# Moving the small tables of a one-core transformer kernel so that the two operands of its split matrix products start at addresses with related remainders

## What is computed

```python
# first kind, twice
proj = rmsnorm(x) @ w_in                       # 1024 -> 4896
y = attention parts of proj
x = x + (gated y @ w_o_fox, w_o_nsa) @ w_out
x = x + square(relu(rmsnorm(x) @ w_up)) @ w_down   # 1024 -> 4096 -> 1024
# second kind, twice (even: MLA + GLA heads; odd: grouped-query heads)
h = x @ w_in_even   or   x @ w_in_odd
x = layer_norm(alpha * x + mixer(h) @ w_o)
ffn = 16 experts of width 1024, each on 64 chosen tokens
ple = sigmoid(x @ ple_gate_w + b) * (p @ ple_w)
x = layer_norm(alpha * x + ffn + ple)
```

## Time and profile before

| what | value |
|---|---|
| median of 3 runs | 3397.64 us |
| the profiled execution, its own time | 3401.32 us |
| its span, first to last instruction | 3399.5 us |
| PE busy | 3210.6 us, 94% of the span |
| DVE, ACT, POOL busy | 38%, 28%, 7% |
| mean granted TensorE clock | 0.975 of full speed |

### The profile page before, as it was taken

The page is one execution under the profiler, slowest core; times in us unless marked ns, Lnnn a source line. Parts: engine busy times, 40 slices in busy tenths (PEclk is TensorE's granted clock), DMA queues, the critical chain, the costliest instruction groups (busy, mean ns, idle before and its releaser), DMA issues. The chain is left out here.

```text
span 3399.5 us, 39981 instructions
## 1 busy us (share of the span) xinstructions
PE 3210.6 (94%) x16110; PEld 2170.6 (64%) x16110; DVE 1286.3 (38%) x1773; ACT 958.2 (28%) x1570; POOL 236.9 (7%) x361
## 2 busy tenths in 40 slices
PE   7999999999999999999997899999997999999996
PEld 5886678888787667888786465444436556544442
DVE  4425554242532564333366552111116655111112
ACT  3325433132422633323242521000004542100001
POOL 1004200000100410000000200000000320000000
PEclk9999999999999999999997999999998999999999
DMA  5310123321441022323211235999992113799997
GB/s 158 119 55 26 66 85 98 99 87 62 130 137 38 1 88 86 99 88 98 77 49 23 76 112 218 426 427 427 427 422 86 64 54 118 304 426 427 427 427 308
DMA packets 234295, 590.22 MB, mean 174 GB/s; under 512 B 42962, under 2 KB 146328, under 8 KB 184996
## 3 DMA queue, kind: packets, MB, share of 16 engines
q1 hardware_dynamic: 234148, 588.15, 45.8%
HBM read 581.81 MB, written 2.10 MB: 172 GB/s over the span
## 5 line engine op out<-in xcount | busy, mean ns | idle before, releaser
L2574 PE MATMUL ps<-w_ring,xe 128*64 128x512 f32 x1024 | 233.7, 602 | 18.8 <-DMA w_ring<-in_w 13.8
L422 DVE TENSOR_TENSOR mlp_w_lo<-w_ring,mlp_w_hi 128x2048 fp32r<-128x2048 f32 x62 | 142.1, 2292 | 212.7 <-ACT mlp_w_hi L382 212.7
L357 PE MATMUL ps<-h_hi,in_w_hi 128*128 128x512 f32 (+1 forms) x528 | 207.0, 392 | 2.7 <-DVE h_lo L430 2.7
L357 PE MATMUL ps<-h_lo,in_w_hi 128*128 128x512 f32 (+1 forms) x528 | 205.7, 390 | 0.0
L357 PE MATMUL ps<-h_hi,in_w_lo 128*128 128x512 f32 (+1 forms) x528 | 205.6, 389 | 0.0
L357 PE MATMUL ps<-h_hi,mlp_w_hi 128*128 128x512 f32 x512 | 202.6, 396 | 2.1 <-DVE h_lo L430 2.1
L357 PE MATMUL ps<-h_hi,mlp_w_lo 128*128 128x512 f32 x512 | 202.5, 396 | 0.0
L357 PE MATMUL ps<-h_lo,mlp_w_hi 128*128 128x512 f32 x512 | 202.5, 395 | 0.0
L357 PE MATMUL ps<-mlp_w_hi,u_lo 128*128 128x512 f32 x512 | 202.3, 395 | 0.0
L357 PE MATMUL ps<-mlp_w_lo,u_hi 128*128 128x512 f32 x512 | 202.2, 395 | 0.0
L357 PE MATMUL ps<-mlp_w_hi,u_hi 128*128 128x512 f32 x512 | 202.2, 395 | 0.0
(11 more groups left out here) (551 smaller groups left out, 6153.2 us busy)
## 6 DMA issues: line engine op xcount, KB each, us to landing
ex_front<-in_w SPq DMA_DIRECT2D x192, 1024.0 KB, 17.5
w_ring<-in_w SPq DMA_DIRECT2D x128, 1024.0 KB, 20.7
ex_back<-in_w SPq DMA_DIRECT2D x64, 1024.0 KB, 19.8
w_ring<-in_w_in SPq DMA_DIRECT2D x32, 1024.0 KB, 5.4
w_ring<-in_w_up SPq DMA_DIRECT2D x32, 1024.0 KB, 5.4
w_ring<-in_w_down SPq DMA_DIRECT2D x32, 1024.0 KB, 5.0
w_ring<-in_cmp_w SPq DMA_DIRECT2D x16, 512.0 KB, 5.0
w_ring<-in_w_out SPq DMA_DIRECT2D x8, 1024.0 KB, 6.0
```

The costliest lines, as they stand in the source:

```text
L357: mm = pe.matmul(ps[0:o.rows, bank[k], 0:o.cols], lhsT, rhs, start=(o.first and j == 0), stop=(o.final and j == len(o.mm) - 1))
L422: dve.tensor_tensor(w.lo[:, home(n), 0:used], ring.slots[:, n % RING, 0:used], w.hi[:, home(n), 0:used].bitcast(F32), ALU.subtract).then_i ...
L2574: mm = pe.matmul(ps[rows, bank + half, :], lhsT, slot(2 * m + a)[:, kk, 512 * half:512 * half + 512], start=(k == 0), stop=(k == DC - 1))
```

## The change

Small tables are padded or put together into one tensor, so that the large pairs behind them start elsewhere. In the lines quoted as in the diff: `n2_tables` grows from 32 to 2048 bytes; the even layer's small tables become slices of one tensor of 512 bytes, `e_small`; the odd layer's become slices of one of 2048 bytes, `o_small`; a tensor that nothing uses, `rw_gap` of 192 bytes, is put ahead of `pl_w`. No instruction is added, removed or moved on any engine; the operands have other addresses.

```diff
@@ block1_layer
-        gain = ctx.enter_context(sbuf(nc, "n2_tables", [P, DC], F32))
-        gemm(nc, "mlp", ps, ring, tiles, 2, nxt, rms_flips(C, I["norm_mlp"][l], h, ring, gain[:, :]), side=tail)
+        gain = ctx.enter_context(sbuf(nc, "n2_tables", [P, BANK], F32))
+        gemm(nc, "mlp", ps, ring, tiles, 2, nxt, rms_flips(C, I["norm_mlp"][l], h, ring, gain[:, 0:DC]), side=tail)
@@ even_beside
-    gw, gb, reset = sb("gw", [2 * GRANK, 2, 256]), sb("gb", [P, 2, 2]), sb("la_reset", [P, T])
+    gw, gb, reset = sb("gw", [2 * GRANK, 2, 256]), small[:, 32:36].rearrange("p (d c) -> p d c", d=2), sb("la_reset", [P, T])
...
-    tot, dec = sb("tot", [P, 2, 2, T // GC]), sb("dec", [P, 2, 2, T // GC])
+    tot, dec = (small[:, c:c + 32].rearrange("p (c d n) -> p c d n", c=2, d=2) for c in (64, 96))
@@ even_mixer
-            gains, add, back = sb("mla_g", [P, 3], c2), sb("add2", [P, 3, 2], c2), sb("back2", [2, 3, P], c2)
+            small, back = sb("e_small", [P, P], c2), sb("back2", [2, 3, P], c2)
+            gains, add, gain = small[:, 0:3], small[:, 8:14].rearrange("p (n m) -> p n m", m=2), small[:, 16:16 + DC]
...
-                gain = sb("nf_gain", [P, DC], c3)
@@ heads_beside
-    gains, ones, back = sb("gqa_g", [P, 2]), sb("add3", [P, 4]), sb("back3", [8, 4, P])
+    small, back = sb("o_small", [P, BANK]), sb("back3", [8, 4, P])
+    gains, ones, rk = small[:, 0:2], small[:, 4:8], small[:, 32:64].rearrange("p (i h) -> p i h", i=TT)
...
-    rk, rs = sb("on_rk", [P, TT, 8]), pair(nc, ctx, "on_rs", [8, T])
+    rs = pair(nc, ctx, "on_rs", [8, T])
@@ route_beside
     rws = pair(nc, ctx, f"rws{i}", [P, DC, NE])
+    sb("rw_gap", [P, 48])
```

More of the change, by code:

```diff
@@ L1441, in _, with even_beside @@
                     pe.matmul(ps[:, 1 + n % 7, :], back_r[:, n, :], rs.lo[:, :], start=False, stop=True).then_inc(s.spread, 1)
-def even_beside(nc, ctx, ps, C, I, x, ring, n_split, cq, ckv, cs, gq, gk, lr, og, gains, add, back):
+def even_beside(nc, ctx, ps, C, I, x, ring, n_split, cq, ckv, cs, gq, gk, lr, og, small, gains, add, back):
     def sb(name, shape, dt=F32):
@@ L1928, in even_mixer @@
             gv, gr, lr = sb("gv", [P, TT, 512], c2), sb("gr", [P, TT, 512], c2), sb("lr", [2 * GRANK, T], c2)
-            side = even_beside(nc, c2, ps, C, I, x, ring, lambda n: 4 + n, cq, ckv, cs, gq, gk, lr, og, gains, add, back)
+            side = even_beside(nc, c2, ps, C, I, x, ring, lambda n: 4 + n, cq, ckv, cs, gq, gk, lr, og, small, gains, add, back)
             with ExitStack() as c3:
@@ L1949, in even_mixer @@
                 tiles += [tokens(E[n] + 256 * m, dst[:, :, 256 * m:256 * m + 256]) for n, dst in (("gv", gv), ("gr", gr)) for m in range(2)]
-                gain = sb("nf_gain", [P, DC], c3)
                 with nc.allow_non_contiguous_dma("narrow columns"):
-                    gemm(nc, "ei", ps, ring, tiles, 2, lead=rms_flips(C, I["norm_final"], h, ring, gain[:, :]), also=tables,
+                    gemm(nc, "ei", ps, ring, tiles, 2, lead=rms_flips(C, I["norm_final"], h, ring, gain), also=tables,
                          side=side, banks=4)
```

## The result

The changed kernel takes 3375.86 us (median of 7 runs, 3368.91 to 3382.67), the kernel before 3397.64 us (7 runs). The ratio is 0.9935, with a 95% interval of 0.9922 to 0.9948: 21.8 us, 0.65%, faster, and clear of the half per cent that the prediction set as its bound.

The account below looks back on a forecast made before the run. The prediction took PE, busy 94% of the span, as the bound; 20.3 + 1.2 - 1.3 + 0.6 - 0.2 + 1.2 = 21.8 us saved from 3397.64 gave 3376 us. The range was 3366 to 3390.

Parts of the forecast that it names:

- the half per cent that the prediction set as its bound: Whole kernel: a measurement can tell about 0.5%, 17.0 us, from no change.
- PE bounds mlp, and its pace is the distance of the operands: mlp: PE busy 358.58 of 358.60 us; 233.3 ns a matmul at distance 32 falls to 226.7 at 0.
- The term of 20.3 us: mlp, two layers: 3072 matmuls each save 233.3 - 226.7 ns once n2_tables is padded, 20.3 us.
- upper bound, 21.8 us: mlp: the most its 3072 matmuls could save, taking wy's 226.2 ns as the aligned pace.
- the first rival: Whole kernel: distance doesn't matter, mlp's 233.3 ns has another cause, time stays at 3398 us; chance 0.08.
- ei about nothing: ei: from distance 32 to 0, wide matmuls save 1.2 us and narrow ones lose 1.3.
- oi and pl: oi: wide matmuls save 0.6 us, narrow ones lose 0.2; pl: saves 1.2 us, bounds 0 and 1.2.
- The partial case, 229.1 ns in mlp: mlp and ei fall only to the pace of oi and pl: 12.2 us saved, 3385 us; chance 0.08.
- No effect: Whole kernel: operand distance doesn't matter at all, the time stays at 3398 us; chance 0.08.
- the slower case: Narrow matmuls lose 1.3 us in ei and 0.2 in oi, mlp gains nothing: 3399 us; chance 0.03.
- Clock by chance, carried by the range: Between stages: pauses of PE lower the granted clock and may shift; the range carries the runs' 13.4 us spread.
- The two small terms that were too large: oi and pl: wide matmuls save 2.4 ns each, 0.6 us in oi and 1.2 us in pl.

Follow-up runs that it names:

- e1: The kernel before with n2_tables padded to 2048 bytes and nothing else: 3378.5 us, ratio 0.9942.
- e5: Changed kernel, mlp activations shifted 32 bytes; weights at equal remainder (first layer), 32 bytes off (second): first mlp as fast as with the change, second as slow as before.
- e7: Changed kernel with n2_tables at 256 bytes in the first layer and 1024 in the second: both mlp stages as good as with 2048.
- e4: Changed kernel with n2_tables at 96 bytes in the first layer, 192 in the second: mlp 358.6 to 359.4 us at 96, 357 us at 192.
- e10: Changed kernel without the gate's bias matmul in pl: pl's steps average 228.1 ns, where it was 228.8 with the bias.
- e13: Changed kernel with an extra 32-column product ahead of mlp outputs opening a PSUM bank, first layer only: first mlp 355.8 us, second 348.5.
- e3: Changed kernel with n2_tables at 64 bytes in the first layer and 128 in the second: mlp 355.3 us at 64, 358.3 us at 128.
- e6: Changed kernel with 32 bytes between hi and lo of mlp's split weights, hi aligned in the first layer, lo in the second: mlp 358.6 and 356.9 us.
- e12: Changed kernel with split weights of 256-column tiles starting 32 bytes later and the experts' ye moved to selT_now's remainder: 3376.35 us, ratio 0.9945.

## Why the prediction was right, point by point

- **PE bounds mlp, and its pace is the distance of the operands.** Right, and shown: e1 has 0.9942 from one table, e5 excludes the operands' own starts, e7 a modulus of 2048. The term of 20.3 us was 20.3 us in the profile. Its upper bound, 21.8 us, came of a reading that was too low: over the starts in wy's stretch of the earlier trace rows a step takes 226.7 ns and not 226.2. What the prediction did not have is that away from 0 one distance can run at two paces (e4). The Trainium skill says in "TensorE: Matmul & The Clock Gate", section "Step-by-step: what each phase is for", that loading the next weights takes no read bandwidth from the running matmul. No run here measures that bandwidth, but what the first rival drew from it, that the distance of the two operands doesn't matter, does not hold for these fp32r streams: 233.3 and 226.7 ns at the same clock differ by the distance alone.
- **ei about nothing.** Right for the steps. The wide ones went from 233.2 to 227.3 ns, the narrow ones from 117.8 to 120.6 (averages over the stage's steps of up to 260 ns): 192 x 5.9 = 1.1 us saved, 384 x 2.8 = 1.1 lost. The stage got 2.0 us shorter all the same, because the clock no longer fell in it; the prediction has no such term.
- **oi and pl.** Mis-sized. The sum has 2.4 ns per wide product, 0.6 and 1.2 us; the averages fell from 229.0 to 228.1 and from 229.3 to 228.8 ns, which gives 0.2 us each. The step that failed is that a short stream would run at 226.7 ns like the long ones of the earlier trace rows. Five to ten steps after each interruption are slower, and these stages are interrupted all the time (e10, e13). The prediction compared the listed distances 64 and 192 as if they were two; counted from the moving to the stationary operand both are 192.
- **The partial case, 229.1 ns in mlp.** Didn't come: at distance 0 mlp went to 226.7 ns. The level itself is real, and mlp showed it at 192 (e3, e4), but it is a pace of that distance and not a floor that something else in mlp sets.
- **No effect, and the slower case.** Excluded by e1 and e5. The narrow products do pay at distance 0, as that rival said, but 1.1 us in ei against 20.3.
- **Clock by chance, carried by the range.** Right as far as it goes: the profile is 3.7 us better than the sum. GLA and ei gave 10.0 us at a higher clock, attention and wy took 5.8 at a lower one, and the rest is small pieces. That the clock moved by chance alone is not shown for GLA and ei.
- **The total.** 3376 forecast, 3375.86 measured. The two small terms that were too large, 0.4 + 1.0 us, are well inside the scatter of the runs, so the agreement to a tenth is luck.

## What to carry to other kernels

Where two operands of a long, unbroken stream of 512-column fp32r products stand at different remainders modulo 256 bytes, look at the distance from start to start, not at the listed durations, and pad the small tensor between them; here a table of 32 bytes cost 20 us. Expect little of it where the stream is broken every dozen products (0.5 to 0.9 ns of 2.4 here), and a small loss where products have 256 columns. One stage at two distances, in two layers of the same run, answers such a question without timing noise; read it in parts in which each operand keeps its role, since a stage's mean can hide two paces.

## What the runs showed of the hardware that was not expected

- The fast pace is a settled state. At distance 0 modulo 256 a stream takes five to ten steps of 224 to 240 ns after the interruptions seen here, then 226, 227, 227 for as long as it lasts. At other distances it falls into other patterns and stays at 228.9 to 234.3 ns on average over a quarter of mlp, at 233.3 in most of them.
- The sign of the distance counts: 192 bytes from the moving to the stationary start gave 228.9 ns, 64 gave 233.3 (e3, e4). And one distance can have two paces: at 192 bytes the up products ran at 228.9 ns and, later in the same stage, at 233.3 (e4).
- One product of three off by 32 bytes slows all three steps: 232.1, 239.0, 228.7 ns (e6). Why the settled states exist, what chooses among them, and why 226.7 ns and no less, these runs don't show.
- Products of 256 columns average 120.6 ns at distance 0 in ei and 117.8 at 32 bytes (e12): for them distance 0 is the slower one.
- The GLA stretch with the same code and tables came at 53 or at 61 us, with a granted clock of 0.84 or 0.75 (the change and e10); a single profile should not be read for 8 us there.
